# Two decoder layers in fp32r pairs on one core: the second layer's key strip ahead of its scores, and four token sums moved from VectorE to GpSimd

## The chip, the core and the metric

The kernel runs on 1 core of a Trainium2 chip. The metric is the device time of one execution in microseconds (us), median of several runs. Engines: TensorE (PE, its weight loads PEld), VectorE (DVE), ScalarE (ACT), GpSimd (POOL), SyncE (SP, which issues nearly all DMAs).

## The reference

528 tokens (16 meta tokens and 512 of the sequence) of width 1024 go through a gated linear attention layer, then through a forgetting-attention (FoX) layer of 16 heads with head width 128. Only the second layer matters here:

```python
k, v, f_logit = jnp.split(rmsnorm(h, kv_norm_g) @ w_kv, [D_INNER, 2 * D_INNER], axis=-1)
cum = jnp.cumsum(jax.nn.log_sigmoid(f_logit + b_forget), axis=1)
q, r = jnp.split(rmsnorm(h, norm_g) @ w_in, 2, axis=-1)
s = jnp.einsum('bhqd,bhkd->bhqk', q, k)          # per head, queries x all earlier keys
s = s + cum[:, :, start:end, None] - cum[:, :, None, :end]
p = jax.nn.softmax(jnp.where(causal, s, NEG_INF), axis=-1)
o = jnp.einsum('bhqk,bhkd->bhqd', p, v)
h = h + (o * jax.nn.silu(r)) @ w_out
```

## The kernel before, in words

**Numbers.** A matrix is held as a pair of fp32r tensors, high and low: ScalarE copies it to fp32r (`hi`), VectorE subtracts this from the original (`lo`), and TensorE adds three products, hi x hi, hi x lo, lo x hi (`project` L1862, `product` L2238). Weights come by DMA in strips of 128 x 1024 into `raw` (a ring of 6), `w_hi` (ring of 4) and `w_lo` (ring of 6); `split` is ScalarE's copy (L625) and VectorE's subtraction (L1128), and `split_to(name)` on either engine does all strips up to that one. The order of all strips is written out in `CHUNKS`, that of TensorE's jobs in `JOBS`.

**The second layer, per head h.** Every engine runs its own list of instructions in order, and semaphores join them. Weight strips are kh (keys), rh and qh (gate and queries) and, for the heads 2 to 13, eh (sums of weight halves). For those heads (`strassen(h)`) r and q are made in one go from seven products of halves (a Strassen scheme). It needs, once, sums of the four quarters of the normalised tokens: `x11`, `x12` are the first half of the features for the first and the second half of the tokens, `x21`, `x22` the second half of the features. `t_raw` (in the memory of `y`) holds the four sums, `t_hi` (ScalarE L996, in the memory of `y_lo`) and `t_lo` (VectorE, `token_sums_lo`) their pair.

TensorE, head h of these: scores (`fox_scores` L2184 to L2186, 15 matmuls for queries x keys), key strip k(h+1) (`key_part`, 48 matmuls), the first three products of head h+1, transposes of the probabilities of h (L2197, L2202), three more products (`middle_products`), `fox_attend(h)` (L2216, L2218), the last product. In the heads 4, 8 and 12 four of the strip's eight feature tiles go before the scores; `n` in the loop over heads says how many. Before heads 4, 8 and 12 there is also a group of value strips u (L2157) and the meta tokens' values (L2121).

VectorE, in the same head: maxima of the scores (L1569, L1576), splits of r, q and e, the scaling of the probabilities (L1597), the key strip's result (`fox_key` L1475), `fk_lo`, `a_lo` (`probs_lo`), the sums of the products (`first_sums`, `second_sums`: `sq`, `y`, `acc` from `psum`), `fox_out` (`sq<-psum,sq`), `fq_lo` (`summed_queries_lo`), the split of k, the weight sums for the head after next (L1501, L1503). The function that lists it is the loop `for h in range(H)` in the VectorE block. The scores wait for `qlo_made` (`fq_lo`), `klo_made`, `alo_made` and `fy_made` (`fox_out`).

GpSimd adds the causal mask to the forget sums (`mask_sums`, L575, four pieces a head) and does two of the weight sums (L599, L601; for head 2 all four, L584 to L590).

**The change-over.** Between the two layers VectorE normalises the tokens (`norm`, L1142, `y<-x2g,rstd`, signals `x2_normed`), takes their low half (`norm_lo`, `x2l<-y,x2h`), joins the meta tokens' values (`end_values_sum`, `ends`), splits k1, q0, r0 and q1, and makes the four token sums in two pairs, `token_sums(False)` before `queries_lo(0)` and `token_sums(True)` behind it. ScalarE's copies `t_hi` wait for all four (`t_made`), and behind them on ScalarE stand the split of r1 and the softmax of head 0. TensorE goes through `fox_values(0)`, strip k1, strip q0, half of strip r0, the scores of head 0, the rest of r0, strip q1, the transposes of head 0 and strip r1.

Of the kernel before, what the change touches and what calls it, by code (L numbers as in the profile page):

```python
# [4 lines left out]
F32 = mybir.dt.float32  # L5
# [72 lines left out]
VH = 4  # L78
# [20 lines left out]
def strassen(h):  # L99

    return S0 <= h < NS
# [100 lines left out]
def program(nc, xT, consts, vecs, w_low, w_up, w_all, w_f, out, rows_out):  # L202
    with ExitStack() as c:
# [362 lines left out]
        @block.gpsimd  # L566
        def _(pool):
            nc.gpsimd.memset(y_lo[0:R_ALL, 12:15, :].bitcast(F32), 0.0).then_inc(g_stack_zeroed, 1)
            pool.wait_ge(cst_loaded, 16)

            def mask_sums(h):
                for b in range(NBLK):
                    pool.wait_ge(sub_loaded[b], 16 * (h + 1))
                    diag = sub[:, SUB_AT[b] + KEYS[b] - BLK:SUB_AT[b] + KEYS[b]]
                    nc.gpsimd.tensor_tensor(diag, diag, above, ALU.add).then_inc(sub_made, 1)  # L575

            def first_weight_sums():
                r, q, e = (CHUNK[f"{x}{S0}"] for x in "rqe")
                w11, w12 = raw[:, r % LO_RING, 0:CH // 2], raw[:, r % LO_RING, CH // 2:CH]
                w21, w22 = raw[:, q % LO_RING, 0:CH // 2], raw[:, q % LO_RING, CH // 2:CH]  # L580
                s2, s4 = raw[:, e % LO_RING, 0:CH // 2], raw[:, e % LO_RING, CH // 2:CH]
                for n in (r, q):
                    pool.wait_ge(w_loaded[n % LO_RING], 16 * LOADS[n])
                nc.gpsimd.tensor_tensor(s1_raw[:], w21, w22, ALU.add).then_inc(sum_made, 1)  # L584
                pool.wait_ge(sum_made, 1)
                nc.gpsimd.tensor_tensor(w21, w21, w11, ALU.add).then_inc(sum_made, 1)
                wait_chunk_used(pool, e - LO_RING)
                nc.gpsimd.tensor_tensor(s2, s1_raw[:], w11, ALU.add).then_inc(sum_made, 1)
                pool.wait_ge(sum_made, 3)
                nc.gpsimd.tensor_tensor(s4, s2, w12, ALU.add).then_inc(sum_made, 1)  # L590

            def later_weight_sums(h):
                i = h - S0
                r, e = CHUNK[f"r{h}"], CHUNK[f"e{h}"]
                w11, w12 = raw[:, r % LO_RING, 0:CH // 2], raw[:, r % LO_RING, CH // 2:CH]
                s2, s4 = raw[:, e % LO_RING, 0:CH // 2], raw[:, e % LO_RING, CH // 2:CH]
                pool.wait_ge(sum_made, 4 * i + 2)
                wait_chunk_used(pool, e - LO_RING)
                nc.gpsimd.tensor_tensor(s2, s1_raw[:], w11, ALU.add).then_inc(sum_made, 1)  # L599
                pool.wait_ge(sum_made, 4 * i + 3)  # L600
                nc.gpsimd.tensor_tensor(s4, s2, w12, ALU.add).then_inc(sum_made, 1)  # L601

            mask_sums(0)
            first_weight_sums()
            for h in range(FOX_HEADS):
                if h + 1 < FOX_HEADS:
                    mask_sums(h + 1)
                if S0 < h + 2 < NS:
                    later_weight_sums(h + 2)

        @block.scalar
        def _(act):
# [380 lines left out]
            queries_hi(0)  # L993
            act.wait_ge(t_made, 4)
            for n in range(4):
                nc.scalar.activation(t_hi[:, n], t_raw[:, n], ACT.Copy).then_inc(thi_made, 1)  # L996
            for h in range(H):
                g = fox_group(h)
                if h + 1 < H and strassen(h + 1):
# [120 lines left out]
        def _(dve):  # L1120
# [500 lines left out]
                tt(x2n[:, 4 * n:4 * n + 4, :], x2g[:, 4 * n:4 * n + 4, :], rstd[:, META:T].rearrange("p (a n) -> p a n", a=1).to_broadcast([P, 4, SEQ]),  # L1621
                   ALU.mult, x2_normed)

            x11, x12, x21, x22 = quarter(x2n, 0, 0), quarter(x2n, 0, 1), quarter(x2n, 1, 0), quarter(x2n, 1, 1)

            def token_sums(late):
                if not late:
                    dve.wait_ge(x2_normed, 2)
                    tt(t_raw[:, 0], x11, x12, ALU.subtract, t_made)
                    dve.wait_ge(t_made, 1)  # L1630
                    nc.vector.scalar_tensor_tensor(t_raw[:, 1], t_raw[:, 0], -1.0, x22, op0=ALU.mult, op1=ALU.subtract).then_inc(t_made, 1)
                else:
                    dve.wait_ge(sums_kept, 16)
                    tt(t_raw[:, 2], x22, x12, ALU.subtract, t_made)
                    dve.wait_ge(t_made, 2)
                    nc.vector.scalar_tensor_tensor(t_raw[:, 3], t_raw[:, 1], -1.0, x21, op0=ALU.mult, op1=ALU.subtract).then_inc(t_made, 1)

            def token_sums_lo(n):
                dve.wait_ge(thi_made, n + 1)
                tt(t_lo[:, n], t_raw[:, n], t_hi[:, n].bitcast(F32), ALU.subtract, tlo_made)  # L1640

            def norm_lo(n):
                dve.wait_ge(x2h_made, n + 1)
# [34 lines left out]
            end_values_lo(0)  # L1678
            fox_values_lo(0)
            split_to("r0")  # L1680
            token_sums(False)
            queries_lo(0)
            token_sums(True)
            split_to("q1")

            for h in range(H):
                g = fox_group(h)
                if h + 1 < H and strassen(h + 1):
# [16 lines left out]
                    first_sums(n)  # L1705
                    second_sums(n)
                    if g is None:
                        fox_out(h)
                        summed_queries_lo(n)
                        split_to(f"k{n + 1}")  # L1710
                        if strassen(h + 2):
                            weight_sums(h + 2)
                    else:
# [135 lines left out]
        def _(pe):  # L1849
# [425 lines left out]

            for h in range(H):

                n = 4 if h % VH == 0 else 0 if strassen(h) else 2
                if h == 0:
                    pe.wait_ge(rtok_made, 4)  # L2280
                    pe.wait_ge(cum_made, 1)
# [185 lines left out]
```

## Time and profile before

| | |
|---|---|
| median of 3 runs | 1016.07 us (1014.77 to 1017.39) |
| the profiled execution | 1014.55 us, its span 1012.8 us |
| busy: TensorE, VectorE, ScalarE, GpSimd | 1001.6, 692.7, 537.1, 84.4 us |
| mean granted TensorE clock | 0.999 of full |
| DMA | 104.00 MB, mean 103 GB/s |

The span goes from the first to the last instruction; the execution's own time has 1.75 us more around it. All places below are in us from the start of the span. The second layer's change-over lies at about 474 to 520, its heads 1 to 15 from there to about 925.

### The profile page before, as it was taken

Reading aid. Unit: us, or ns where it says so; the run is one execution under the profiler, and the core shown is the slowest. Engines: PE = TensorE matmul, PEld = TensorE weight load, DVE = VectorE, ACT = ScalarE, POOL = GpSimd, SP = SyncE. Lnnn points to the kernel's source line nnn. Section 1 sums busy time; section 2 is a strip of 40 time slices with the busy share of each in tenths; the row PEclk is TensorE's granted clock in tenths of the full one; section 3 lists DMA queues with packets and bytes.
Section 4 is the critical chain, followed back from the end, with each engine's and each line's share of the span. In section 5 each row is a group of like instructions: output and inputs, shape, how many; then the busy total and the mean of one; then the engine's idle time right before and its main releaser. Section 6 shows DMA issues by size and latency. Waiting matters only on the chain.

```text
span 1012.8 us, 18920 instructions
## 1 busy us (share of the span) xinstructions
PE 1001.6 (99%) x7699; PEld 937.9 (93%) x7699; DVE 692.7 (68%) x1140; ACT 537.1 (53%) x900; POOL 84.4 (8%) x95
## 2 busy tenths in 40 slices
PE   9999999999999999999999999999999999999998
PEld 8999999999999999997779989999899989988887
DVE  6875667577567784337889875888588866775332
ACT  6754654564464554226475555556465645674332
POOL 0000000000000000000132202212122311100000
PEclk9999999999999999999999999999999999999999
DMA  8221221221122114332334533444245523743412
GB/s 290 82 66 63 83 86 43 83 84 64 63 84 84 64 42 131 131 104 75 131 80 103 112 130 75 116 102 152 84 104 115 136 91 111 238 108 118 143 52 83
DMA packets 40375, 104.00 MB, mean 103 GB/s; under 512 B 4560, under 2 KB 12624, under 8 KB 40288
## 3 DMA queue, kind: packets, MB, share of 16 engines
q1 hardware_dynamic: 39568, 102.11, 33.3%
q8 instruction: 61, 1.00, 0.4%
q10 hardware_dynamic: 720, 0.68, 0.2%
q14 instruction: 26, 0.21, 0.1%
HBM read 94.94 MB, written 7.64 MB: 101 GB/s over the span
## 4 chain that ended last, share of the span: by engine, by line
PE 92%; DVE 4%; ACT 2%; issue 1%; DMA 0%; DVEq 0%; ACTq 0%
PE psum L1862 57%; PE psum L2238 12%; PE psum L2157 7%; PE psum L2216 3%; PE psum L1987 2%; PE psum L2197 2%; PE psum L1935 1%; PE psum L2184 1%; PE psum L1983 1%; PE psum L2185 1%; PE psum L2186 1%; PE psum L1956 1%; PE psum L2121 1%; PE psum L1915 1%; DVE w_lo L1128 1%
## 5 line engine op out<-in xcount | busy, mean ns | idle before, releaser
L1128 DVE TENSOR_TENSOR w_lo<-raw,w_hi 128x1024 fp32r<-128x1024 f32 x155 | 189.4, 1237 | 45.2 <-ACT w_hi L625 34.9
L625 ACT ACTIVATE w_hi<-raw 128x1024 fp32r<-128x1024 f32 x155 | 161.6, 1051 | 32.5 <-PE psum L2157 29.5
L1862 PE MATMUL psum<-xh,w_hi 128*128 128x264 f32 x768 | 159.2, 288 | 0.2 <-DVE w_lo L1142 0.2
L1862 PE MATMUL psum<-xl,w_hi 128*128 128x264 f32 x768 | 155.9, 285 | 0.0
L1862 PE MATMUL psum<-xh,w_lo 128*128 128x264 f32 x768 | 155.3, 283 | 0.0
L1862 PEld LDWEIGHTS psum<-xh,w_hi 128*128 128x128 f32 x768 | 118.7, 189 | 1.5 <-issue 1.4
L1862 PEld LDWEIGHTS psum<-xl,w_hi 128*128 128x128 f32 x768 | 119.5, 188 | 0.0
L1862 PEld LDWEIGHTS psum<-xh,w_lo 128*128 128x128 f32 x768 | 119.1, 188 | 0.0
L1862 PE MATMUL psum<-y_lo,w_hi 128*128 128x264 f32 (+2 forms) x400 | 104.8, 314 | 0.0
L575 POOL TENSOR_TENSOR sub<-sub,cst 128x128 f32<-128x128 f32 x64 | 47.3, 740 | 656.2 <-DMA sub<-sums 655.8
L1862 PEld LDWEIGHTS psum<-y_lo,w_hi 128*128 128x128 f32 x400 | 66.7, 188 | 4.6
L1142 DVE TENSOR_TENSOR hT<-psum,hT 128x528 f32<-128x528 f32 (+2 forms) x17 | 11.3, 667 | 71.1 <-PE psum L1862 71.1
L2238 PE MATMUL psum<-y_lo,w_hi 128*128 128x256 f32 x288 | 53.4, 287 | 0.1
L1862 PE MATMUL psum<-z_hi,w_hi 128*128 128x512 f32 (+1 forms) x144 | 53.1, 369 | 0.0
L1862 PE MATMUL psum<-z_hi,w_lo 128*128 128x512 f32 (+1 forms) x144 | 52.8, 367 | 0.0
L1862 PE MATMUL psum<-zh,w_hi 128*128 128x264 f32 x256 | 52.3, 285 | 0.0
L1862 PE MATMUL psum<-y_hi,w_hi 128*128 128x264 f32 x256 | 52.0, 284 | 0.0
L1862 PE MATMUL psum<-zl,w_hi 128*128 128x264 f32 x256 | 52.0, 285 | 0.0
L1862 PE MATMUL psum<-y_hi,w_lo 128*128 128x264 f32 x256 | 51.8, 284 | 0.0
L1862 PE MATMUL psum<-zh,w_lo 128*128 128x264 f32 x256 | 51.8, 283 | 0.0
L2157 PE MATMUL psum<-w_hi,zh 128*128 128x512 f32 x128 | 51.0, 398 | 0.0
L2157 PE MATMUL psum<-w_hi,zl 128*128 128x512 f32 x128 | 50.6, 395 | 0.0
(323 smaller groups left out, 2375.1 us busy)
## 6 DMA issues: line engine op xcount, KB each, us to landing
raw<-w_all SPq DMA_DIRECT2D x143, 512.0 KB, 3.3
sub<-sums SPq DMA_DIRECT2D x16, 264.0 KB, 7.2
y_keep<-sq SPq DMA_DIRECT2D x13, 256.0 KB, 2.2
y<-y_keep SPq DMA_DIRECT2D x13, 256.0 KB, 6.3
sub<-sums SPq DMA_DIRECT2D x16, 200.0 KB, 6.3
sub<-sums SPq DMA_DIRECT2D x16, 136.0 KB, 4.8
hT<-xT SPq DMA_DIRECT2D x8, 264.0 KB, 5.6
h_keep<-hT SPq DMA_DIRECT2D x8, 256.0 KB, 4.1
```

Of the source, the lines that this page charges most:

```text
L575: nc.gpsimd.tensor_tensor(diag, diag, above, ALU.add).then_inc(sub_made, 1)
L625: nc.scalar.activation(w_hi[:, n % HI_RING, :], raw[:, n % LO_RING, :], ACT.Copy).then_inc(hi_made, 1)
L1128: nc.vector.tensor_tensor(w_lo[:, n % LO_RING, :], raw[:, n % LO_RING, :], w_hi[:, n % HI_RING, :].bitcast(F32), ALU.subtract).then_inc(lo ...
L1142: nc.vector.tensor_tensor(out, a, b, op).then_inc(made, 1)
L1862: i = nc.tensor.matmul(o, w[a][:, k % KT, :], x[b][:, k, c0:c1], start=k == first and a == b == 0, stop=k == last and a == 1)
L1915: i = nc.tensor.transpose(bank(x + 1, b * P, (b + 1) * P), src[:, b * P:(b + 1) * P], ident)
L1935: i = nc.tensor.matmul(out, lhs[:, t], rhs[:, t], start=t == 0, stop=t == CT - 1)
L1987: nc.tensor.matmul(bank(x + 1, 400 - w, 400), vs[a][:, j, :], gs[b][:, A_DIAG[j]:A_DIAG[j] + w], start=False, stop=False)
L2157: i = nc.tensor.matmul(bank(4 + b), xk[a][:, k, b * BLK:(b + 1) * BLK], w[p][:, k % 2, :], start=k == a == p == 0, stop=k == KT - 1 and a ...
L2197: nc.tensor.transpose(bank(bk, c0, c0 + BLK), pr[b][:, BLK * j:BLK * j + BLK], ident)
L2216: nc.tensor.matmul(bank(slot(job), PT_Q0[j], SEQ), vs[a][:, j, v], ps[b][:, AF_AT[j]:AF_AT[j] + w], start=j == 0 and a == b == 0, stop=False)
L2238: i = nc.tensor.matmul(o, w[a][:, k0 + k, :], x[b][:, k, :], start=k == a == b == 0, stop=k == KT // 2 - 1 and a == 1)
```

## The change

Four things. In the Strassen heads other than 4, 8 and 12, two of the key strip's eight tiles now go before the scores (`n` 2, was 0). On VectorE the split of that key strip goes before `fox_out` and `fq_lo`. The four token sums leave VectorE and are the first work of GpSimd in the second layer. And the second of them is kept with the other sign, so that it is a plain addition and the fourth a plain subtraction; ScalarE's copy and VectorE's low half turn the sign back.

```diff
@@ GpSimd, ahead of its masks and weight sums @@
+            x11, x12, x21, x22 = quarter(x2n, 0, 0), quarter(x2n, 0, 1), quarter(x2n, 1, 0), quarter(x2n, 1, 1)
+            pool.wait_ge(x2_normed, 2)
+            nc.gpsimd.tensor_tensor(t_raw[:, 0], x11, x12, ALU.subtract).then_inc(t_made, 1)
+            pool.wait_ge(t_made, 1)
+            nc.gpsimd.tensor_tensor(t_raw[:, 1], t_raw[:, 0], x22, ALU.add).then_inc(t_made, 1)
+            pool.wait_ge(sums_kept, 16)
+            pool.wait_ge(cum_done, 1)
+            nc.gpsimd.tensor_tensor(t_raw[:, 2], x22, x12, ALU.subtract).then_inc(t_made, 1)
+            pool.wait_ge(t_made, 2)
+            nc.gpsimd.tensor_tensor(t_raw[:, 3], t_raw[:, 1], x21, ALU.subtract).then_inc(t_made, 1)
             mask_sums(0)
             first_weight_sums()
@@ ScalarE @@
             for n in range(4):
-                nc.scalar.activation(t_hi[:, n], t_raw[:, n], ACT.Copy).then_inc(thi_made, 1)
+                nc.scalar.activation(t_hi[:, n], t_raw[:, n], ACT.Copy, scale=-1.0 if n == 1 else 1.0).then_inc(thi_made, 1)
@@ VectorE @@
-            def token_sums(late):
-                if not late:
-                    dve.wait_ge(x2_normed, 2)
-                    tt(t_raw[:, 0], x11, x12, ALU.subtract, t_made)
-                    dve.wait_ge(t_made, 1)
-                    nc.vector.scalar_tensor_tensor(t_raw[:, 1], t_raw[:, 0], -1.0, x22, op0=ALU.mult, op1=ALU.subtract).then_inc(t_made, 1)
-                else:
-                    dve.wait_ge(sums_kept, 16)
-                    tt(t_raw[:, 2], x22, x12, ALU.subtract, t_made)
-                    dve.wait_ge(t_made, 2)
-                    nc.vector.scalar_tensor_tensor(t_raw[:, 3], t_raw[:, 1], -1.0, x21, op0=ALU.mult, op1=ALU.subtract).then_inc(t_made, 1)
             def token_sums_lo(n):
                 dve.wait_ge(thi_made, n + 1)
-                tt(t_lo[:, n], t_raw[:, n], t_hi[:, n].bitcast(F32), ALU.subtract, tlo_made)
+                if n == 1:
+                    nc.vector.scalar_tensor_tensor(t_lo[:, n], t_raw[:, n], -1.0, t_hi[:, n].bitcast(F32), op0=ALU.mult, op1=ALU.subtract).then_inc(tlo_made, 1)
+                else:
+                    tt(t_lo[:, n], t_raw[:, n], t_hi[:, n].bitcast(F32), ALU.subtract, tlo_made)
...
             split_to("r0")
-            token_sums(False)
             queries_lo(0)
-            token_sums(True)
             split_to("q1")
...
                     if g is None:
+                        split_to(f"k{n + 1}")
                         fox_out(h)
                         summed_queries_lo(n)
-                        split_to(f"k{n + 1}")
@@ TensorE @@
-                n = 4 if h % VH == 0 else 0 if strassen(h) else 2
+                n = 4 if h % VH == 0 else 2
```

How the instructions stand, at two places. On VectorE, before head 3's scores (`fox_out` is `sq<-psum,sq`, the split of k4 `w_lo<-raw,w_hi`); before the change:

```order
L1142 TENSOR_TENSOR acc<-psum,acc 128x256
L1142 TENSOR_TENSOR sq<-psum,sq 128x512
L1142 TENSOR_TENSOR fq_lo<-acc,fq_hi 128x512
L1128 TENSOR_TENSOR w_lo<-raw,w_hi 128x1024
L1501 TENSOR_TENSOR s_raw<-raw 128x512
```

and with it:

```order
L1152 TENSOR_TENSOR acc<-psum,acc 128x256
L1138 TENSOR_TENSOR w_lo<-raw,w_hi 128x1024
L1152 TENSOR_TENSOR sq<-psum,sq 128x512
L1152 TENSOR_TENSOR fq_lo<-acc,fq_hi 128x512
L1511 TENSOR_TENSOR s_raw<-raw 128x512
```

The split has moved from behind `fq_lo` to ahead of `fox_out`. (All line numbers of the VectorE block are 10 higher in the changed kernel.)

On GpSimd, from its first work of the second layer on, before the change:

```order
L568 MEMSET y_lo 80x1584
L575 ISA
L575 TENSOR_TENSOR sub<-sub,cst 128x128 x4
L584 TENSOR_TENSOR s_raw<-raw 128x512
L586 TENSOR_TENSOR raw<-raw 128x512
```

and with it:

```order
L568 MEMSET y_lo 80x1584
L605 ISA
L605 TENSOR_TENSOR y<-y 128x1024
L607 TENSOR_TENSOR y<-y 128x1024
L610 TENSOR_TENSOR y<-y 128x1024
L612 TENSOR_TENSOR y<-y 128x1024
L575 TENSOR_TENSOR sub<-sub,cst 128x128 x4
L584 TENSOR_TENSOR s_raw<-raw 128x512
```

The four token sums stand ahead of the masks of head 0 and of the first weight sums.

## Rows read from the trace of the kernel before

**Rows 1.** The page's part 1: busy us, share of the span, instructions
```profile
PE 1001.6 (99%) x7699; PEld 937.9 (93%) x7699; DVE 692.7 (68%) x1140; ACT 537.1 (53%) x900; POOL 84.4 (8%) x95
```
**Rows 2.** Waits of TensorE: line, releaser, us in total, times, longest
```profile
PE psum L2184 <- issue: 1.5, 9, 0.2
```
**Rows 3.** Timeline, TensorE, head 3: start, length, operation, [idle before <-releaser]
```profile
571.87 0.28 PE L2238 MATMUL psum<-x2h,w_lo 128*128 128x256 f32 x1
572.34 0.30 PE L2184 MATMUL psum<-fk_hi,fq_hi 128*128 128x144 f32 x1 [0.19 <-issue]
```
**Rows 4.** Timeline, VectorE, same place: fox_out, fq_lo, split of k4
```profile
570.66 0.69 DVE L1142 TENSOR_TENSOR sq<-psum,sq 128x512 f32<-128x512 f32 x1 [1.50 <-PE psum L2218]
571.26 0.68 DVE L1142 TENSOR_TENSOR fq_lo<-acc,fq_hi 128x512 fp32r<-128x512 f32 x1
571.86 1.22 DVE L1128 TENSOR_TENSOR w_lo<-raw,w_hi 128x1024 fp32r<-128x1024 f32 x1
```
**Rows 5.** Timeline, TensorE, head 4: end of the strip's first four tiles, scores
```profile
621.08 0.40 PE L1862 MATMUL psum<-zh,w_lo 128*128 128x264 f32 x2
621.32 0.23 PE L2184 MATMUL psum<-fk_hi,fq_hi 128*128 128x144 f32 x1
```
**Rows 6.** Timeline, VectorE, change-over, 481 to 512
```profile
481.88 2.29 DVE L1142 TENSOR_TENSOR y<-x2g,rstd 128x2048 f32<-128x2048 f32 x1
487.10 1.23 DVE L1128 TENSOR_TENSOR w_lo<-raw,w_hi 128x1024 fp32r<-128x1024 f32 x1 [2.93 <-ACT w_hi L625]
488.24 2.56 DVE L1142 TENSOR_TENSOR x2l<-y,x2h 128x2048 fp32r<-128x2048 f32 x1
...
491.50 1.46 DVE L1142 TENSOR_TENSOR ends<-ends 16x512 f32<-16x512 f32 x2
492.89 2.27 DVE L1142 TENSOR_TENSOR x2l<-y,x2h 128x2048 fp32r<-128x2048 f32 x1
...
506.67 2.31 DVE L1636 SCALAR_TENSOR_TENSOR y<-y 128x1024 f32<-128x1024 f32 x1
508.91 2.31 DVE L1128 TENSOR_TENSOR w_lo<-raw,w_hi 128x1024 fp32r<-128x1024 f32 x1
```
**Rows 7.** Timeline, GpSimd, change-over
```profile
484.72 0.46 POOL L575 TENSOR_TENSOR sub<-sub,cst 128x128 f32<-128x128 f32 x1 [482.57 <-DMA sub<-sums]
...
507.98 2.16 POOL L586 TENSOR_TENSOR raw<-raw 128x512 f32<-128x512 f32 x1
...
512.45 1.30 POOL L590 TENSOR_TENSOR raw<-raw 128x512 f32<-128x512 f32 x1
```
**Rows 8.** Timeline, ScalarE, change-over
```profile
493.07 1.47 ACT L919 ACTIVATE fv_end<-ends,rtok 16x512 fp32r<-16x512 f32 x2 [6.01 <-DVE ends L1142]
494.57 2.00 ACT L625 ACTIVATE w_hi<-raw 128x1024 fp32r<-128x1024 f32 x2
...
509.02 3.91 ACT L996 ACTIVATE y_lo<-y 128x1024 fp32r<-128x1024 f32 x4 [5.55 <-DVE y L1636]
```
**Rows 9.** Timeline, TensorE, change-over: k1, q0, q1, transposes of head 0, r1
```profile
490.02 0.41 PE L1862 MATMUL psum<-zh,w_hi 128*128 128x264 f32 x2
...
496.99 0.47 PE L1862 MATMUL psum<-x2h,w_hi 128*128 128x512 f32 x1 [0.96 <-issue]
...
511.27 0.50 PE L1862 MATMUL psum<-x2h,w_hi 128*128 128x512 f32 x1 [0.53 <-DVE w_lo L1128]
...
518.40 1.28 PE L2197 MATMUL psum<-cst,pr 128*128 128x128 f32 x10 [1.26 <-DVE pr L1597]
...
520.44 0.50 PE L1862 MATMUL psum<-x2h,w_hi 128*128 128x512 f32 x1 [0.42 <-ACT sq L945]
```
**Rows 10.** TensorE alone: timeline at the start; stretch at the end (length, busy, PEclk, DMA)
```profile
1.06 5.49 PE L1993 MATMUL psum<-zeros 128*128 128x128 f32 x24 [1.06 <-DVE eps L1150]
1.00:7.00 6.00, 5.73 (x25) 1.00 0.88 277
1008.00:1012.80 4.80, 0.00 (x1) 0.78 0.69 257
```

More of the change, by code:

```diff
@@ L1622, in norm @@
                    ALU.mult, x2_normed)
-            x11, x12, x21, x22 = quarter(x2n, 0, 0), quarter(x2n, 0, 1), quarter(x2n, 1, 0), quarter(x2n, 1, 1)
-            def token_sums(late):
-                if not late:
-                    dve.wait_ge(x2_normed, 2)
-                    tt(t_raw[:, 0], x11, x12, ALU.subtract, t_made)
-                    dve.wait_ge(t_made, 1)
-                    nc.vector.scalar_tensor_tensor(t_raw[:, 1], t_raw[:, 0], -1.0, x22, op0=ALU.mult, op1=ALU.subtract).then_inc(t_made, 1)
-                else:
-                    dve.wait_ge(sums_kept, 16)
-                    tt(t_raw[:, 2], x22, x12, ALU.subtract, t_made)
-                    dve.wait_ge(t_made, 2)
-                    nc.vector.scalar_tensor_tensor(t_raw[:, 3], t_raw[:, 1], -1.0, x21, op0=ALU.mult, op1=ALU.subtract).then_inc(t_made, 1)
             def token_sums_lo(n):
                 dve.wait_ge(thi_made, n + 1)
-                tt(t_lo[:, n], t_raw[:, n], t_hi[:, n].bitcast(F32), ALU.subtract, tlo_made)
+                if n == 1:
+                    nc.vector.scalar_tensor_tensor(t_lo[:, n], t_raw[:, n], -1.0, t_hi[:, n].bitcast(F32), op0=ALU.mult, op1=ALU.subtract).then_inc(tlo_made, 1)
+                else:
+                    tt(t_lo[:, n], t_raw[:, n], t_hi[:, n].bitcast(F32), ALU.subtract, tlo_made)
             def norm_lo(n):
```

## The prediction

> **What bounds the kernel now.** I read the page's shares first: TensorE is busy for 99% of the span [rows 1]. So nothing is won by making another engine faster in itself; time can only come from, or go into, the places where TensorE stands still. The list of waits has one entry that repeats: the first score matmul (L2184) has idle time before it 9 times, 1.5 us in all [rows 2]. The timeline shows what such a place is and how to price it: the last matmul of `last_product` starts at 571.87, the first score matmul at 572.34 [rows 3]. Matmuls of this width start 0.12 us apart, so 0.47 - 0.12 = 0.35 us of starts are lost where the view prints 0.19: a printed idle time has to be raised by 0.16, since a matmul (0.28 us) lies over its successors. Nine such places cost 1.5 + 9 x 0.16 = 2.95 us.
>
> Their cause is on VectorE. `fox_out` waits 1.50 us for `fox_attend`, then takes 0.69, and `fq_lo`, which the scores read, follows and ends at 571.26 + 0.68 = 571.94 [rows 4]; TensorE, which has run out of `last_product` at about that time, then works through its waits. In head 4, where four of the key strip's eight tiles stand before the scores, the first score matmul starts 0.24 us after the last pair of strip matmuls began, the distance of any such pair: no loss [rows 5].
>
> The other waits lie in the change-over to the second layer: 0.96, 0.53, 1.26 and 0.42 us as printed, 1.12, 0.69, 1.42 and 0.58 with the 0.16 [rows 9].
>
> **Part one, the order of key strip and scores (9 heads).** TensorE does the same matmuls; 12 of them (1.46 us at 0.12) now stand between `last_product` and the scores. They need the low half of strip k (VectorE, 1.22 us), which used to come after `fq_lo`, at 571.86, and now comes before `fox_out`. There VectorE sat idle for 1.50 us [rows 4], so the split fits with 0.3 us to spare, and `fox_out` and `fq_lo` keep their times. `fq_lo` is then ready about 1.4 us before the scores want it. Gain: all of the 2.95 us; the other end is 0, if the wait only moves. What is late next: the scores end 1.46 - 0.33 = 1.1 us later after `last_product`, and the maxima wait for them; but with the split gone from behind `fq_lo` VectorE itself comes to its maxima 1.2 us sooner, so it meets the scores and the softmax isn't later. I cost it at nothing; if it were short, the transposes of the probabilities would wait next, by the 1.1 us at most.
>
> **Part two, four token sums on GpSimd.** VectorE loses four operations of 1.2 us (the last took 2.31 [rows 6]). On GpSimd I have 0.46 us for 128 columns and 1.30 for 512 [rows 7]: 2.2 ns a column and 0.18 fixed, so 2.4 us for 1024 columns, the four 9.6 us. Twice the 512 row would be 2.6, the upper end of a plain reading; both rows have unbroken operands, while these read four pieces of 256. The Trainium skill, "GPSIMD Engine Reference", section "3. Performance versus the Vector engine", gives 4497 ns for an add of 2048 columns; half of that is an estimate of 2.25 us, which would make the stall below 0.45 us shorter. No run here shows that size.
>
> Where they land decides. They wait for `x2_normed` (set by the operation that ends at 481.88 + 2.29 = 484.2 [rows 6]) and don't wait for anything later, so they start at once and fill 484.2 to about 497. What is queued behind them on GpSimd, `mask_sums(0)`, is wanted only from 511 on. But VectorE is needed there, and the trace shows what the two engines do to each other: the GpSimd sum at 507.98 took 2.16 us instead of 1.30, and the VectorE operations at 506.67 and 508.91 took 2.31 instead of 1.22, and the latter ends at 511.22, 1.1 us, its own length, after GpSimd's ended at 510.14 [rows 6, 7]. The first `x2l`, met by a 0.46 us GpSimd operation, took 2.56, the second 2.27. So an operation with two SBUF inputs waits for the other engine's whole operation, and they alternate. The Trainium skill, "SBUF — State Buffer", section "SBUF: two separate sides", states it as a lock held for the full instruction whatever its length; the rows here show it for 512 columns. If a longer one were instead let in between, the sum would be the one of the second rival.
>
> I replay it. VectorE idles until 487.10 (2.93 us, waiting for `w_hi`), so the first sum (484.3 to 486.7) costs nothing. The second (486.8 to 489.2) holds up the split of k1: 489.2 to 490.3; TensorE wants k1 at 490.0 [rows 9], 0.3 us late, which the next stall covers. Third sum to 492.6, first `x2l` to 494.8, fourth sum to 497.1; the two `ends` additions of 0.7 each and the pieces of `mask_sums` between them end at 498.7 (before: 492.96). From there the chain is that of before: ScalarE's `fv_end` pair 1.47 and the split of q0, half of 2.00 [rows 8], then `w_lo` of q0 on VectorE 1.22, with the second `x2l` beside them. TensorE can start q0 at about 502.7 instead of 496.99: **+5.7 us**. The bounds: 0 if VectorE always wins the race, 7.2 + 1.4 (three sums and four mask pieces, all on the path) = 8.6 if it always loses and nothing is covered.
>
> What the four removals give back, behind that place. VectorE comes to the split of q1 2.4 us before TensorE needs it, where it now ends at 511.22: -0.69. The maxima no longer stand behind it, and ScalarE's four `t_hi` copies, which waited 5.55 us for the last sum [rows 8], start right after q0's copy; the softmax then ends over 3 us before the transposes want it: -1.42. The gate (ScalarE L945) is early too: -0.5 of 0.58, as 0.1 stays at this place in later heads. Sum -2.6; the other end is 0.
>
> A stall of 5.4 us before q0 has a second price, the clock. At the end of the span TensorE does nothing from 1008.0 to 1012.8, and the granted clock of that stretch is 0.78 [rows 10]: full for 2.7 us, then at its lower level, half (1.2 GHz). The way back is seen only at the start: 24 matmuls of 128 columns took 5.49 us, 0.23 apart [rows 10], against 0.12 for the transposes (10 in 1.28 us [rows 9]), though the granted clock reads 1.00 there. So the cost lies between 0 and half of 5.5, 2.7 us; neither row is nearer to this case, so I take 1.4. The Trainium skill, "TensorE: Matmul & The Clock Gate", section "What's actually happening", has the clock at half after idleness and full again after sustained work; it would put the cost above 0, not at 0.
>
> **Sum**: +5.7 - 2.6 - 2.95 + 1.4 = +1.55, rounded +1.5 us. The profiled execution took 1014.55 us (span 1012.8 and 1.75 around it), so it would take 1016.1. It lies 1.5 below the median of the three runs, 1016.07; the forecast, and the rivals' times, are given against that median: **1017.6 us**. About 0.3% (3 us) is what a measurement of this kernel can tell from no change, so this is "the same".
>
> **The rivals.**
> 1. *As forecast, but the clock stays up* or is back at once: +0.1, 1016.2. For it: only the idle time, and nothing that was done in it, is known from one place, and the fall may come when the stall is nearly over. Against it: the fall at the end.
> 2. *The engines don't block each other over these sums*, or VectorE wins most races: no stall, and -2.6 - 2.95 = -5.55, 1010.5. For it: no row has a GpSimd operation of this length beside VectorE, and here VectorE has more to do; against it the two rows of 2.31.
> 3. *The strided sums are slow on GpSimd* (slower than before): each of the three blocking sums adds its excess to the stall. At 3.3 us instead of 2.4 that is +2.7, 1020.3. It decides from 2.9 us a sum on, where the total passes +3. For it: no row has such operands; against it: on VectorE the fourth sum, with the same operands, took the 2.31 of the plain split behind it [rows 6].
> 4. *The score wait only moves*, because the strip's low half is late or the waits cost what they cost now wherever they stand: the 2.95 is not won, 1020.5. Against it: head 4.
>
> **How the numbers follow.** The forecast (stall and clock) 0.40, rival 1 0.20, rival 2 0.20, rival 3 0.13, rival 4 0.07. Faster by over 0.3% is rival 2: 0.20. Same is the forecast and rival 1: 0.60. Slower is rivals 3 and 4: 0.20. The range 1010.5 to 1020.3 goes from rival 2 to rival 3; mixtures (VectorE wins one race, one of the gains misses) lie inside. The likeliest cases alone span 1016 to 1018.5.
>
> **What would show it.** In the changed profile: four GpSimd operations on y of about 2.4 us from 484.3 on, the later ones stretched; k1's split and `x2l` near 3.2 and 4.7 us on VectorE; TensorE's idle time before q0 about 6.5 us instead of 0.96, with the granted clock under 1.00 behind it; no printed waits before q1, before the transposes of head 0 and after them; none of the nine entries before the first score matmul. I am wrong if q0 starts before 500 (rival 2), if a sum takes over 2.9 us alone (rival 3), or if the first score matmul still has idle time before it (rival 4).

## The result and the profile after

The changed kernel takes 1017.40 us (median of 20 executions, 1016.40 to 1018.16), the kernel before 1014.97 (20 executions, 1013.12 to 1017.51): ratio 1.0024, 95% interval 1.0017 to 1.0031, that is 2.4 us slower (1.7 to 3.1). The prediction called anything under 0.3% "the same"; 20 executions of each kernel do tell this difference from none. The median lies 0.2 us under the forecast. The profiled execution took 1016.83 us (span 1015.0), 2.28 more than that of before.

The page's part 1 (busy us, share, instructions) answers to [rows 1]: TensorE does the same 7699 matmuls, GpSimd has the four sums, VectorE four operations fewer, and yet VectorE's busy time rose from 692.7 to 694.9.

```profile
PE 999.2 (98%) x7699; PEld 937.4 (92%) x7699; DVE 694.9 (68%) x1136; ACT 539.5 (53%) x900; POOL 95.1 (9%) x99
```

TensorE's waits of the changed kernel (line, releaser: total, times, longest). The nine before the first score matmul [rows 2] are gone, and one of 6.0 us stands there that was 0.96 [rows 9]. The second line is new: the transposes of the probabilities, once.

```profile
PE psum L1859 <- DVE w_lo L1138: 6.2, 2, 6.0
PE psum L2194 <- DVE pr L1607: 1.5, 1, 1.5
...
PE psum L2235 <- DVE w_lo L1138: 0.4, 1, 0.4
```

The change-over, where the 6.0 us come from. GpSimd's timeline (start, length; L605 to L612 are the four sums, L575 the mask pieces):

```profile
484.61 2.41 POOL L605 TENSOR_TENSOR y<-y 128x1024 f32<-128x1024 f32 x1 [482.46 <-DVE y L1152]
487.11 2.41 POOL L607 TENSOR_TENSOR y<-y 128x1024 f32<-128x1024 f32 x1
489.47 3.38 POOL L610 TENSOR_TENSOR y<-y 128x1024 f32<-128x1024 f32 x1
492.81 4.43 POOL L612 TENSOR_TENSOR y<-y 128x1024 f32<-128x1024 f32 x1
497.20 5.77 POOL L575 TENSOR_TENSOR sub<-sub,cst 128x128 f32<-128x128 f32 x4
```

VectorE's timeline beside it, to be laid against [rows 6]:

```profile
487.39 3.20 DVE L1138 TENSOR_TENSOR w_lo<-raw,w_hi 128x1024 fp32r<-128x1024 f32 x1 [2.93 <-ACT w_hi L635]
490.52 4.48 DVE L1152 TENSOR_TENSOR x2l<-y,x2h 128x2048 fp32r<-128x2048 f32 x1
494.92 0.67 DVE L1152 TENSOR_TENSOR ends<-psum,ends 16x512 f32<-16x512 f32 x1
495.70 2.94 DVE L1152 TENSOR_TENSOR ends<-ends 16x512 f32<-16x512 f32 x2
498.57 2.27 DVE L1152 TENSOR_TENSOR x2l<-y,x2h 128x2048 fp32r<-128x2048 f32 x1
501.34 1.32 DVE L1138 TENSOR_TENSOR w_lo<-raw,w_hi 128x1024 fp32r<-128x1024 f32 x1 [0.50 <-ACT w_hi L635]
```

Read the two together. A sum takes 2.41 us where nothing is in its way (the first: VectorE idles). The split of k1 has 1.2 us of work and is recorded with 3.20, from 487.39 to 490.59: 1.1 us, about its own length, after the second sum's end at 489.5. `x2l` (2.27 of work) ends at 495.0, 2.2 us after the third sum's end at 492.85. And the fourth sum ends 2.2 us after `x2l`: the two engines alternate, each record holding the wait and then the work.

TensorE's timeline: the start of q0, and the matmuls of 512 columns behind it, which start 0.43 us apart up to 505.5 and then 0.23 apart.

```profile
496.35 0.41 PE L1859 MATMUL psum<-zh,w_lo 128*128 128x264 f32 x2
502.76 0.77 PE L1859 MATMUL psum<-x2h,w_hi 128*128 128x512 f32 x1 [6.00 <-DVE w_lo L1138]
503.32 0.63 PE L1859 MATMUL psum<-x2l,w_hi 128*128 128x512 f32 x1
503.75 0.63 PE L1859 MATMUL psum<-x2h,w_lo 128*128 128x512 f32 x1
...
505.45 0.57 PE L1859 MATMUL psum<-x2h,w_hi 128*128 128x512 f32 x1
505.86 0.39 PE L1859 MATMUL psum<-x2l,w_hi 128*128 128x512 f32 x1
```

Part one shows in head 3. The pair before the scores starts at 577.22, the first score matmul 0.24 us later and without idle time, where [rows 3] lost 0.35:

```profile
577.22 0.40 PE L1859 MATMUL psum<-zh,w_lo 128*128 128x264 f32 x2
577.46 0.23 PE L2181 MATMUL psum<-fk_hi,fq_hi 128*128 128x144 f32 x1
```

But in head 13, the last with summed weights, VectorE stands still before its maxima, and TensorE then waits for the probabilities. VectorE, then TensorE, changed kernel:

```profile
865.29 0.42 DVE L1152 TENSOR_TENSOR sq<-psum,y 128x256 f32<-128x256 f32 x1 [0.24 <-PE psum L2235]
867.48 0.77 DVE L1579 SCALAR_TENSOR_TENSOR pr<-sub,cum_t,psum 128x144 f32<-128x144 f32 x2 [1.77 <-PE psum L2183]
```
```profile
874.54 1.28 PE L2194 MATMUL psum<-cst,pr 128*128 128x128 f32 x10 [1.46 <-DVE pr L1607]
```

In head 3 VectorE has two `weight_sums` operations (L1511, L1513) between `fq_lo` and the maxima; no head behind 13 needs any, so here nothing covers that the scores come 1.1 us later.

**The ledger.** How much later than before the same instruction of TensorE starts, in profiled executions; each column is reduced by its kernel's lead or lag at strip k0 (464.74 before), which no kernel touches and which varies by up to 0.9 us between executions. The columns are the kernels of the next section.

| start of | after | e1 | e2 | e3 | e4 | e5 | e6 | e8 | e10 | c1 | c2 |
|---|---|---|---|---|---|---|---|---|---|---|---|
| strip q0 (496.99) | +5.48 | -0.28 | +5.46 | +5.46 | -0.28 | +1.69 | -0.28 | -0.28 | +5.47 | -0.28 | -0.28 |
| scores, head 0 (505.72) | +6.61 | -0.28 | +7.09 | +7.35 | +4.47 | +3.48 | -0.03 | +4.27 | +5.65 | +3.07 | -0.28 |
| transposes, head 0 (518.40) | +4.32 | -0.30 | +4.79 | +5.06 | +2.18 | +1.19 | -2.32 | +2.28 | +3.36 | +0.78 | -0.76 |
| `fox_attend`, head 0 (524.75) | +3.81 | +1.27 | +4.27 | +4.54 | +1.66 | +0.66 | -2.83 | +1.77 | +2.83 | +0.26 | +0.78 |
| the same, head 1 (546.45) | +4.10 | +1.28 | +4.54 | +4.75 | +1.92 | +0.88 | -2.62 | +1.77 | +2.84 | +0.59 | +1.07 |
| the same, head 11 (814.43) | +0.84 | -1.99 | +4.58 | +1.49 | -1.34 | -2.40 | -5.89 | -1.50 | -0.42 | -2.69 | -2.21 |
| the same, head 13 (879.53) | +1.97 | -0.94 | +4.76 | +1.45 | -0.23 | -1.29 | -4.85 | -1.55 | +0.57 | -2.69 | -2.29 |
| last matmul (1007.73) | +1.99 | -0.92 | +4.79 | +1.44 | -0.20 | -1.27 | -4.84 | -1.48 | +0.59 | -2.63 | -2.27 |

For the change itself: +5.48 up to q0, +1.13 to the scores, -2.29 and -0.51 to head 0's attend, +0.29 in head 1, -3.26 in eight heads up to head 11 (0.41 each), +1.13 in head 13.

### The profile page after: what moved, and what is told of

It is laid out like the page before. It is cut to its first block, busy times and chain, and to the rows that moved or that the text cites. A ratio compares the mean times of both kernels' runs of the same rounds, so it can differ in the third digit from the quotient of the medians.

```text
span 1015.0 us, 18921 instructions
## 1 busy us (share of the span) xinstructions
PE 999.2 (98%) x7699; PEld 937.4 (92%) x7699; DVE 694.9 (68%) x1136; ACT 539.5 (53%) x900; POOL 95.1 (9%) x99
## 4 chain that ended last, share of the span: by engine, by line
PE 93%; DVE 3%; issue 1%; ACT 1%; DMA 0%; DVEq 0%; SPq 0%; ACTq 0%
PE psum L1859 58%; PE psum L2235 12%; PE psum L2154 7%; PE psum L2213 3%; PE psum L1984 2%; PE psum L2194 2%; PE psum L1932 1%; PE psum L2182 1%; PE psum L2181 1%; PE psum L2183 1%; PE psum L1980 1%; PE psum L1953 1%; DVE w_lo L1138 1%; PE psum L2118 1%; PE psum L1912 1%
## 5 line engine op out<-in xcount | busy, mean ns | idle before, releaser
L575 POOL TENSOR_TENSOR sub<-sub,cst 128x128 f32<-128x128 f32 x64 | 46.5, 729 | 177.6 <-DMA sub<-sums 177.5
```

## The experiments

**e1, part one alone** (on the kernel before):
```diff
-                n = 4 if h % VH == 0 else 0 if strassen(h) else 2
+                n = 4 if h % VH == 0 else 2
...
+                        split_to(f"k{n + 1}")
                         fox_out(h)
                         summed_queries_lo(n)
-                        split_to(f"k{n + 1}")
```


> Part one alone, on the kernel before: two of the key strip's tiles ahead of the scores in every head and the split of the key strip ahead of fox_out; the four token sums stay on VectorE. Theory of the prediction: the nine waits before the first score matmul go, -2.95 us, nothing else moves: 1012.0 against 1015.0. Theory from the trace of the changed kernel: only eight of the heads win (-3.25 us in all by the places where TensorE's instructions start), and the last head with summed weights gives 1.1 us back before its transposes, because VectorE comes to the softmax late there: -2.1 us, about 1012.9. Rival, that the wait only moves: 1015.0, no change. In all cases q0 starts at 497.0 as before and the granted clock of 497:503 stays 1.00.

Measured: 1012.89 against 1014.69, ratio 0.9980 (0.9971 to 0.9989), -1.8 us (-1.1 to -2.9). The ledger has the eight heads at -3.27 and head 13 at +1.05, as the second theory said; the rival is out. The profiled execution lost 1.57 us more between the transposes and the attend of head 0, a place that the edit doesn't touch: the timeline of TensorE there has the same waits as before (1.25 and 0.42, [rows 9]), but its matmuls of 512 columns then start 0.43 us apart.

```profile
518.12 1.28 PE L2197 MATMUL psum<-cst,pr 128*128 128x128 f32 x10 [1.25 <-DVE pr L1597]
...
520.15 0.76 PE L1862 MATMUL psum<-x2h,w_hi 128*128 128x512 f32 x1 [0.42 <-ACT sq L945]
520.72 0.63 PE L1862 MATMUL psum<-x2l,w_hi 128*128 128x512 f32 x1
521.14 0.63 PE L1862 MATMUL psum<-x2h,w_lo 128*128 128x512 f32 x1
```

The stretch 519 to 522 in e1 and, second fence, before (length; busy time and instructions of PE, PEld, DVE, ACT and POOL; granted clock; DMA share; GB/s):

```profile
519.00:522.00 3.00, 2.58 (x13) 1.89 (x12) 2.29 (x4) 2.95 (x8) 1.50 (x3) 0.70 0.84 261
```
```profile
519.00:522.00 3.00, 2.58 (x18) 2.01 (x17) 2.29 (x4) 2.96 (x6) 1.74 (x3) 1.00 0.93 259
```

**e2, part two alone** (the changed kernel with both edits of e1 taken back):

> Part two alone: the changed kernel with the order of key strip, scores and split put back; the four sums are on GpSimd. Theory of the prediction: +5.7 (q0 late) -2.6 (three waits behind it) +1.4 (clock) = +4.5 us, 1019.5 against 1015.0; the trace of the changed kernel, read place by place, says +4.1 to +4.4. Rival, that the two parts depend on each other (part one wins only because VectorE is freer after part two, or part two's gains come from the new order): +2.4 us or less, since the whole change is +2.4. The nine waits before the first score matmul are back, the wait before q0 is 6.0 us as printed.

Measured: 1019.89 against 1014.69, 1.0053 (1.0040 to 1.0066), +5.2 us (4.1 to 6.7). The nine waits are back in its list (1.5, 9, 0.2). So part one is worth 1.8 us on the kernel before and 2.5 to 2.8 on top of part two (1019.89 to 1017.40, or +5.2 to +2.4 against the kernel before of each series): the parts add up within their intervals, and the change is the sum of a gain and a larger loss.

**e3, head 13 with the old tiles** (on the changed kernel):
```diff
-                n = 4 if h % VH == 0 else 2
+                n = 4 if h % VH == 0 else 0 if h == NS - 1 else 2
```


> The changed kernel, but in the last head with summed weights no tiles of the key strip stand ahead of the scores. Theory: the printed wait of 1.5 us before that head's transposes goes and a wait of about 0.2 before its first score matmul comes back: profiled time 1.1 us below that of the changed kernel, 1015.7. Rival, that the wait comes from the early split of the key strip and not from the tiles: it stays, 1016.8.

One execution: 1016.91 us. The total hides it, since this execution was 0.93 us late already at k0 and lost 0.74 more between q0 and the scores, where its clock stayed low for longer (see the clock below); the ledger shows it: from head 11 to head 13 the changed kernel loses 1.13 us, this one gains 0.04. The wait for `pr` is gone from the list. It also stands at 1.3 to 1.4 us in e1, e4, e5, e6 and e10, which keep the new tiles there, and is missing in e8, c1 and c2, which don't. So it is the tiles, not the earlier split.

**e6, memsets in place of the sums** (the four token sums are left out; GpSimd writes zeros, three times 1024 columns for each sum):
```diff
-            nc.gpsimd.tensor_tensor(t_raw[:, 0], x11, x12, ALU.subtract).then_inc(t_made, 1)
+            for n in range(PIECES):
+                pool.wait_ge(in_order, n + 0 * PIECES)
+                nc.gpsimd.memset(t_raw[:, 0], 0.0).then_inc(in_order, 1)
+            pool.wait_ge(in_order, 1 * PIECES)
+            nc.gpsimd.memset(t_raw[:, 0], 0.0).then_inc(t_made, 1)
...
```


> In place of each of the four token sums GpSimd runs three memsets of the same 1024 columns (about 0.93 us each by the memset of 1584 columns at the start, 1.41 us), so it is busy as long or a little longer but reads nothing from SBUF; the four sums are left out. Theory A (the exclusion needs GpSimd to read SBUF as VectorE does, with two inputs): VectorE's k1 split is back at 1.2 us and x2l at 2.3, the wait before q0 at 1 to 1.5 us, the time near 1011. Theory B (any operation of GpSimd excludes): split and x2l stay stretched by up to 0.9 us each, the wait before q0 2 to 4 us. Theory C (it is not exclusion but GpSimd being late for its own following work, mask_sums): as in the changed kernel, 6 us.

One execution: 1009.69 us. GpSimd is busy without a break from 484.2 to 496.1, and VectorE beside it has its lengths of before. VectorE of e6, then GpSimd:

```profile
487.05 1.23 DVE L1156 TENSOR_TENSOR w_lo<-raw,w_hi 128x1024 fp32r<-128x1024 f32 x1 [2.93 <-ACT w_hi L653]
488.19 2.29 DVE L1170 TENSOR_TENSOR x2l<-y,x2h 128x2048 fp32r<-128x2048 f32 x1
```
```profile
486.26 0.96 POOL L611 MEMSET y<- 128x1024 f32 x1
487.27 1.97 POOL L615 MEMSET y<- 128x1024 f32 x2
```

Theory A holds. The stall isn't GpSimd's load and not the place of `mask_sums`: it needs an operation of GpSimd that reads SBUF. All such operations here have two inputs there; one with a single input was not tried. The Trainium skill, "SBUF — State Buffer", section "SBUF: two separate sides", says of VectorE operations with two SBUF inputs that they take the lock "only against a GpSimd op that reads SBUF"; the row of 1.23 beside the memsets, against 3.20 beside the sums, agrees. The same kernel shows what freeing VectorE is worth if nothing blocks: q0 on time, then -2.29 and -0.51 in head 0, the 2.8 us for which the prediction had 2.6.

**e4, late sums** (on the changed kernel):
```diff
+            pool.wait_ge(lo_made, CHUNK["q0"] + 1)
             pool.wait_ge(t_made, 1)
             nc.gpsimd.tensor_tensor(t_raw[:, 1], t_raw[:, 0], x22, ALU.add).then_inc(t_made, 1)
```


> The changed kernel, but GpSimd's second, third and fourth token sum wait until VectorE has made the low half of q0's weights. Theory (whole operations of the two engines exclude each other, and that alone makes the stall): the wait before q0 falls from 6.0 us to about 1 (the first sum still ends before VectorE's split of k1), the clock stays at 1.00 in 503:506, and the gains behind (no wait before q1, none before the transposes of head 0) stay, since the sums are needed only from 511 on: -4.5 to -5 us against before, 1010. Rival A, that the stall is mainly something else (the scaled copy, the pieces of mask_sums, slow strided operands): the wait before q0 stays over 3 us and the time above 1013. Rival B, the lock bites later: the sums now run beside the VectorE work of 500 to 512 (q1's split, the key split), the stall moves to q1 or to the scores, 1013 to 1015.

Measured: 1014.22 against 1014.69, 0.9993 (0.9984 to 1.0003): no difference that can be told from none, 3.2 us less than the changed kernel. The time is rival B's, the place is one that it didn't name: q0 starts on time and the strip behind it, r0, ahead of q1 and of the scores, waits 3.29 us, and the clock falls behind that wait (0.50 from 506 to 509). VectorE, then GpSimd:

```profile
498.01 2.33 DVE L1559 SCALAR_TENSOR_TENSOR fv_end<-ends,rtok,fv_end 16x512 fp32r<-16x512 f32 x1
500.38 2.73 DVE L1565 SCALAR_TENSOR_TENSOR fv_lo<-psum,rtok,fv_hi 128x512 fp32r<-128x512 f32 x4
503.02 2.98 DVE L1139 TENSOR_TENSOR w_lo<-raw,w_hi 128x1024 fp32r<-128x1024 f32 x1
```
```profile
496.99 2.81 POOL L608 TENSOR_TENSOR y<-y 128x1024 f32<-128x1024 f32 x1 [9.96 <-DVE w_lo L1139]
499.76 2.86 POOL L611 TENSOR_TENSOR y<-y 128x1024 f32<-128x1024 f32 x1
502.58 2.34 POOL L613 TENSOR_TENSOR y<-y 128x1024 f32<-128x1024 f32 x1
```

`fv_end`, on 16 partitions and 0.74 us before, waits for a whole sum as well; the four `fv_lo` that read PSUM take the same 2.73 as before (four from 498.76, the next operation at 501.40) beside a sum that reads SBUF throughout.

**e5, only the third and the fourth late:**

> The changed kernel, but only the third and the fourth sum wait for the low half of q0's weights. Theory of the lock: one sum of 2.4 us (the second) still delays VectorE's split of k1 by 2 us, which TensorE's earlier stall mostly hides; the second x2l operation now starts without waiting: the wait before q0 between 1 and 3.3 us. The granted clock of the stretch behind it tells how short a stall still drops it: 1.00 behind under 2.7 us of idleness (what the end of the span shows), 0.5 if shorter ones drop it too.

One execution: 1013.96 us. The wait before q0 is 2.24 us, as expected for one blocking sum, and the one before r0 0.25 as printed, 0.4 in starts. But the clock fell: 0.51 in 500 to 503. The bound taken from the end of the span, 2.7 us of idleness at full clock [rows 10], doesn't hold in the middle of the kernel.

**e8, e4 and e3 together:**

> As the kernel with the late sums, and in the last head with summed weights no key strip tiles stand ahead of the scores (as before the change). Theory: the wait of 1.5 us before that head's transposes goes, 1.1 us less than the kernel with the late sums: -5.6 to -6 us against before, 1009.2. Rival: that wait has another cause than the 12 matmuls' delay of the scores (VectorE is late in any case): same as the kernel with the late sums, -4.5 to -5.

Measured: 1013.47 against 1014.69, 0.9989 (0.9980 to 0.9998). The step from e4 is -0.75 by the medians and -1.3 by the ledger; the total is far from the -5.6 expected, for e4's reason.

**The clock: e7, e9, e10.** The changed kernel plus matmuls of zeros between the strips k1 and q0, 27 in e7 and 25 in the others, each recorded as two. Their place is the difference. In e7 they stood behind the wait for q0's weights, in e9 behind the one for `x2l`, in e10 ahead of both:
```diff
+            pe.wait_ge(end_sum, 1)
+            for n in range(DUMMY):
+                nc.tensor.matmul(bank(slot("q0"), 0, P), zeros[:], zeros[:], start=True, stop=True)
             pe.wait_ge(x2l_made, 2)
             strip_late("q0", xq)
```


> The changed kernel with 27 matmuls of zeros (128 columns, 0.213 us apart at the start of the span, 5.8 us) into q0's bank, between strip k1 and strip q0: TensorE is busy through most of the 6 us in which it waited. Theory (the clock term: idleness drops the granted clock, and the matmuls of 512 columns behind it run at half speed for a while): the matmuls behind q0's first start 0.213 apart and not 0.427, the granted clock stays 1.00, and the profiled time is 1.1 us below the changed kernel's, 1015.7. Rival: the slow first matmuls of q0 have another cause (operands, PSUM): time and spacing as in the changed kernel, 1016.8.

> The changed kernel with 25 matmuls of zeros into q0's bank, this time ahead of the wait for q0's weights, so that they run inside the stall (two records each, 0.112 apart at full clock as the run with 27 showed, so 5.6 us from 496.7 on). Theory of the clock term: TensorE is never idle for more than a microsecond, the granted clock stays 1.00, the first matmuls of q0 start 0.213 apart instead of 0.427, and the distance from q0's start to the first scores is 8.7 us as before and not 9.87: 1.1 us less than the changed kernel, 1016.3 as a median. Rival: the matmuls behind the stall are slow for another reason (operands just written, both engines' traffic): the distance stays 9.87 and the time 1017.4.

> As the last two kernels with matmuls of zeros, but now the 25 stand right behind the strip k1, ahead of the wait for x2l, which had held them back to 500.99. So TensorE is busy from 496.7 to about 502.3 and q0 starts at about 502.7 as in the changed kernel. Theory of the clock term: granted clock 1.00 from 496 to 506, 8.5 to 8.7 us from q0's start to the first scores instead of 9.87, 1016.3 as a median against 1017.4. Rival: the clock falls although TensorE is busy with zeros, or the stretch stays slow without it: 1017.4, or 1018 where the matmuls of zeros hold q0 up.

e7 (one execution, 1023.67) and e9 (1020.49 against 1014.67) missed their aim: TensorE still idled for 5.99 and 4.13 us, and the zeros came on top. They measured something else. In e9 the zeros start 0.213 us apart up to 505.8 and 0.112 apart from there on, in e7 from 507.1 on, and then q0's matmuls go at 0.23: the slow matmuls behind the stall are slow whatever they multiply. TensorE in e9:

```profile
500.99 8.19 PE L1877 MATMUL psum<-zeros 128*128 128x128 f32 x50 [4.13 <-DVE x2l L1153]
508.93 0.48 PE L1860 MATMUL psum<-x2h,w_hi 128*128 128x512 f32 x1
509.25 0.40 PE L1860 MATMUL psum<-x2l,w_hi 128*128 128x512 f32 x1
509.48 0.40 PE L1860 MATMUL psum<-x2h,w_lo 128*128 128x512 f32 x1
```

e10 is the test: 1015.33 against 1014.90, 1.0006 (0.9996 to 1.0015), 2.1 us less than the changed kernel although q0 is as late as there. From q0 to the scores it takes 8.91 us instead of 9.87. Its zeros start 0.11 us apart from the first on. The same two stretches of e10 and, second fence, of the changed kernel; the granted clock is the third number from the end:

```profile
500.00:503.00 3.00, 2.91 (x27) 2.71 (x25) 2.50 (x2) 2.93 (x5) 3.00 (x3) 1.00 0.03 10
503.00:506.00 3.00, 2.68 (x12) 2.21 (x13) 2.94 (x8) 3.00 (x5) 0.54 (x1) 1.00 0.00 0
```
```profile
500.00:503.00 3.00, 0.24 (x1) 0.28 (x2) 2.50 (x3) 2.95 (x5) 2.97 (x3) 0.50 0.00 0
503.00:506.00 3.00, 3.00 (x8) 2.34 (x9) 2.94 (x8) 2.65 (x4) 0.00 (x0) 0.53 0.00 0
```

**c1, two sums on each engine:** VectorE makes the first two in the 2.93 us in which it waits [rows 6], GpSimd the other two from q0's low half on, head 13 keeps its old tiles:
```diff
-            pool.wait_ge(x2_normed, 2)
-            nc.gpsimd.tensor_tensor(t_raw[:, 0], x11, x12, ALU.subtract).then_inc(t_made, 1)
-            pool.wait_ge(t_made, 1)
-            nc.gpsimd.tensor_tensor(t_raw[:, 1], t_raw[:, 0], x22, ALU.add).then_inc(t_made, 1)
             pool.wait_ge(sums_kept, 16)
             pool.wait_ge(cum_done, 1)
+            pool.wait_ge(lo_made, CHUNK["q0"] + 1)
...
             norm(1)
+            dve.wait_ge(x2_normed, 2)
+            tt(t_raw[:, 0], x11, x12, ALU.subtract, t_made)
+            dve.wait_ge(t_made, 1)
+            tt(t_raw[:, 1], t_raw[:, 0], x22, ALU.add, t_made)
             split_to("k1")
```


> Both lessons: VectorE makes the first two token sums in the 2.93 us in which it stood still before the split of k1 (2.44 us of work, no operation of GpSimd beside it), GpSimd makes the third and the fourth, and starts them only when q0's low half is made; and the last head with summed weights keeps the old order of tiles. Theory (operations of the two engines that read SBUF exclude each other, idle time is free): q0 starts as before the change (497.0), the wait before q1 is about 0.4 us as in the run with two late sums, none before the transposes of head 0, the clock stays at 1.00: -2.2 us from part two and -3.2 from part one, 1009.3 against 1014.7. Rival: the late sums move the stall to q1 as with three late sums (3.5 us and a dip of the clock): 1012.5 to 1013.5.

Measured: 1010.37 against 1014.67, ratio 0.9959 (0.9947 to 0.9972): 4.2 us faster than before (2.8 to 5.4), 7.0 less than the changed kernel. This version beats both. The first two sums are free (2.49 us, the split of k1 starts at 487.25). The expected wait of 0.4 us (put before q1; in e5 it stood before r0) was wrong: r0 waits 1.82, since `fv_end` again stood behind a sum. VectorE, then TensorE:

```profile
484.35 2.49 DVE L1149 TENSOR_TENSOR y<-y 128x1024 f32<-128x1024 f32 x2
487.25 1.23 DVE L1135 TENSOR_TENSOR w_lo<-raw,w_hi 128x1024 fp32r<-128x1024 f32 x1 [0.41 <-ACT w_hi L632]
...
497.86 2.33 DVE L1555 SCALAR_TENSOR_TENSOR fv_end<-ends,rtok,fv_end 16x512 fp32r<-16x512 f32 x1
```
```profile
504.52 0.47 PE L1862 MATMUL psum<-x2h,w_hi 128*128 128x512 f32 x1 [1.82 <-DVE w_lo L1135]
```

**c2, the two sums later still** (on c1): the mask pieces at q0's low half, the sums at r0's.
```diff
             pool.wait_ge(lo_made, CHUNK["q0"] + 1)
+            mask_sums(0)
+            pool.wait_ge(lo_made, CHUNK["r0"] + 1)
...
-            mask_sums(0)
             first_weight_sums()
```


> As the kernel with two sums on VectorE and two on GpSimd, but GpSimd starts its two only when the low half of r0 is made (VectorE has only q1's split and an operation from PSUM to do then), and makes the four mask pieces before them. Theory (the wait of 1.99 us before r0 comes from one operation of VectorE, fv_end, that stood behind GpSimd's third sum, 2.33 us instead of 0.74): r0 starts without a wait, no dip of the clock behind it: 1.9 us less than that kernel's undisturbed executions (1010.1), about 1008.3, -6.4 against before. Rival: the wait moves to q1 (VectorE's split of it stands behind the fourth sum) and then to the maxima: 1009 to 1010.

Measured: 1011.33 against 1014.90, 0.9963 (0.9950 to 0.9976). r0 starts without a wait, and the transposes of head 0 get one of 1.66 us, behind which the clock falls here too (0.52 from 520 to 523), at a cost of 1.54 us in the ledger, from the transposes to the attend of head 0: the last sum ends at 508.66, ScalarE's four `t_hi` copies run behind it, and the exponentials of the softmax stand behind the copies. ScalarE, then TensorE:

```profile
508.69 3.90 ACT L1004 ACTIVATE y_lo<-y 128x1024 fp32r<-128x1024 f32 x4 [5.07 <-POOL y L611]
```
```profile
518.08 1.28 PE L2198 MATMUL psum<-cst,pr 128*128 128x128 f32 x10 [1.66 <-DVE pr L1605]
```

That is the wait of the kernel before [rows 8, 9]. The rival had the right direction; the wait moved one step further than it said. The profiled executions of c1 and c2 are the slowest of their five each, 1.7 and 1.4 us above the median. c1 and c2 can't be told apart by their intervals.

## Why the prediction was right

**The stall, +5.7.** Held: +5.48 in the ledger (q0 at 502.76; the prediction said 502.7). The replay of the two engines was right operation by operation: sums of 2.41 us (2.4 predicted), the split of k1 at 3.20 (near 3.2), `x2l` at 4.48 (near 4.7). e6 shows the premise, exclusion between operations that read SBUF, and not only its consequence. With it rival 2 (no blocking, 1010.5) falls; e6 is what it described, and took 1009.69. Rival 3 (slow strided sums) falls by the first sum: 2.41 us alone.

**The gains behind it, -2.6.** Held in size: -2.29 and -0.51, 2.8 us. One loss in head 1 wasn't foreseen: the first matmul behind the transposes starts 0.54 us after the last of them, where before it was 0.25. That is the 0.29 of the ledger; VectorE's two splits there took 2.86 us (2.62 before), with mask pieces of GpSimd beside them in both kernels. The cause was not tested, and stays open.

**The clock, +1.4.** The mechanism is shown by e10. In the profiled execution of the changed kernel it cost 1.14 us from q0 to the scores (9.87 against 8.73 before), and e10 gets 0.96 of them back. e2 and e3 have the same stall and took 10.35 and 10.62 us there, 1.6 and 1.9 more than before: from 506 to 509 their granted clock is 0.89 and 0.65, where the changed kernel is back at 1.00. So one stall costs a different amount in each execution, and 1.4 lies among the three. By the medians the zeros are worth 2.1 us; the intervals (e10 -0.4 to +1.5, the change +1.7 to +3.1 against before) leave 0.2 to 3.5, which holds all of them. Rival 1 (the clock stays up) falls.

**Part one, -2.95.** The mechanism was right and the sum too high by 0.8: the ledger has -3.26 + 1.13 = -2.1. What failed is the step "with the split gone from behind `fq_lo` VectorE itself comes to its maxima 1.2 us sooner, so it meets the scores ... I cost it at nothing". It holds in eight heads. In head 13 VectorE is early too but has no `weight_sums` to fill the time, and idles 1.77 us; the softmax starts when the scores end, which is later. The sentence behind it, that the transposes would then wait "by the 1.1 us at most", gave the place and the size of that wait; a look at the last head, which the loop `if strassen(h + 2)` sets apart, would have given it to the sum. The eight others won 0.41 each, where the sum of 2.95 had 0.33, and made up for 0.6 of the 1.5 us missing in head 13 (its own 0.33 and the 1.13). Rival 4 (the wait only moves) was true in one head of nine.

**The sum.** Predicted +1.5 between profiled executions, measured +2.28, of which 0.29 lay ahead of k0. That the forecast came within 0.2 us of the median is partly luck: the shown median of three, 1016.07, was 1.1 above the median of 20, and the error in part one went the other way. Two slips did no harm: the upper bound of the stall is 9.0 and not 8.6 (four mask pieces at 0.46 are 1.8, not 1.4), and rival 4's 1020.5 lies just outside the range.

## What to carry to other kernels

Moving work of this kind from VectorE to GpSimd freed VectorE only where its own operations there read PSUM, or where it stood still anyway; beside two-input operations in SBUF each waited for the other's whole length, so long GpSimd operations are worse neighbours than short ones. Operations of VectorE with one tensor in SBUF came out both ways. The reduces for the maxima were not held up (0.42 us for 272 columns beside c2's last sum, as before), but the scaling of the probabilities was: the first two pieces took 1.13 and 1.33 us beside GpSimd's weight sums, against 0.30 and 0.36 before. In the changed kernel:

```profile
518.40 1.13 DVE L1607 TENSOR_SCALAR pr<-pr,inv 128x144 f32<-128x144 f32 x1
519.64 1.33 DVE L1607 TENSOR_SCALAR pr<-pr,inv 128x272 f32<-128x272 f32 x1
```

First look for idle time on the engine that has the work already: here 2.49 us of sums fitted into 2.93 us of VectorE's waiting, at no cost. And when work is put ahead of a consumer in every turn of a loop, check the last turn, where the work that used to cover the delay may be missing.

## What the runs showed of the hardware

- The clock falls after shorter waits than the end of the span suggested, and not every time. Matmuls ran at half rate for 3 to 5 us behind waits (as printed) of 6.0, 4.13, 3.29, 2.24 and 1.82 us, in c2 behind 1.66 and 0.42 close together and in e1 behind 1.25 and 0.42. The kernel before has the pair of 1.26 and 0.42 as well and kept its clock at 1.00 in its profile; and the wait of 1.46 us in head 13, between full stretches of matmuls, left it at 1.00 in the changed kernel, as did those of 1.3 to 1.4 there in seven other profiles.
- The time of one kernel varies with it. Of 52 executions of the kernel before that ran beside the experiments, eight show a mean granted clock of 0.997, and they took 1015.97 to 1017.03 us; the other 44, at 0.998 to 1.000, took 1013.22 to 1015.95. c1 at 0.997 took 1012.07 (that is the profiled one), its other four 1009.75 to 1010.44. All 20 of the changed kernel stand at 0.995 or 0.996. Where in those eight executions the clock fell isn't known, since only their totals were kept. So a stall that the clock outlives most times costs its length, and one that it never outlives costs more: 1.1 to 1.9 us in the three profiles with the wait of 6.0 us.
- The granted clock printed for the first microseconds can mislead: the stretch 1 to 7 reads 1.00 [rows 10], while its matmuls of zeros start 0.23 apart on the mean; e9 shows the same matmuls at 0.213 where the clock reads 0.50, and at 0.112 where it reads 1.00.
